# Two of three modulation rows summed on VectorE instead of TensorE, in a one-core DiT layer

## The reference, cut to what matters

```python
mod = (jax.nn.silu(c) @ w_mod[i] + b_mod[i])[:, None, :]     # 2048 x 12288
sh1, sc1, g1, sh2, sc2, g2 = jnp.split(mod, 6, axis=-1)
h = modulate(rms_norm(x, mix_norm_pre[i]), sh1, sc1)
p = h @ w_in[i]
...
x = x + g1 * rms_norm(mix @ w_out[i], mix_norm_post[i])
hf = modulate(rms_norm(x, ffn_norm_pre[i]), sh2, sc2)
x = x + g2 * rms_norm(swiglu(hf, w_gate[i], w_up[i], w_down[i]), ffn_norm_post[i])
```

## Time and profile before

| | us |
|---|---|
| median of 3 runs | 1610.84 (1610.16 to 1612.67) |
| profiled execution, its own time | 1613.92 |
| its span, first to last instruction | 1612.2 |
| TensorE matmul busy | 1538.3 (95%) |
| VectorE busy | 1033.4 (64%) |
| ScalarE busy | 739.2 (46%) |
| GpSimd busy | 222.2 (14%) |

### The profile page before, as it was taken

How to read it: one execution, slowest core, us unless ns; L and a number is a source line. 1 busy time by engine, 2 the same in 40 slices (tenths; PEclk the granted TensorE clock), 3 DMA queues, 4 the chain that set the end, 5 groups by cost and what they waited for, 6 DMA issues and landing times.

```text
span 1612.2 us, 25110 instructions
## 1 busy us (share of the span) xinstructions
PE 1538.3 (95%) x9297; PEld 1295.0 (80%) x9297; DVE 1033.4 (64%) x1435; ACT 739.2 (46%) x1042; POOL 222.2 (14%) x236
## 2 busy tenths in 40 slices
PE   3888999999999999999999999999999999999998
PEld 0557888898889888898877888888888888888786
DVE  1446899999997766665577544545454454777554
ACT  5535534443345745455357444444444443443332
POOL 2000223333242324244100000000000000000000
PEclk9998999999999999999999999999999999999999
DMA  9994566555655556564373766666666666998653
GB/s 351 382 397 116 167 199 196 190 190 183 208 179 176 171 171 209 170 196 132 118 261 117 212 194 186 192 185 192 184 193 192 187 190 191 339 321 319 222 187 136
DMA packets 190977, 334.58 MB, mean 208 GB/s; under 512 B 14706, under 2 KB 80354, under 8 KB 189985
## 3 DMA queue, kind: packets, MB, share of 16 engines
q1 hardware_dynamic: 190194, 330.89, 63.3%
q0 software_dynamic: 688, 2.39, 0.5%
HBM read 331.15 MB, written 2.10 MB: 207 GB/s over the span
## 4 chain that ended last, share of the span: by engine, by line
PE 82%; DVE 9%; DMA 2%; ACT 2%; SPq 2%; issue 2%; DVEq 0%; ACTq 0%
PE PS L1886 67%; DVE cacc L1752 3%; DMA first<-in_w_mod_dram 2%; DVE w_lo L1465 2%; PE PS L2107 2%; PE PS L2155 2%; PE PS L1892 2%; PE PS L2201 2%; SPq L756 2%; DVE sil L1586 1%; PE PS L2053 1%; PE PS L2097 1%; PE PS L1982 1%; DVE xyi L1645 1%; ACT L973 1%
## 5 line engine op out<-in xcount | busy, mean ns | idle before, releaser
L977 ACT ACTIVATE w_hi<-raw 128x1024 fp32r<-128x1024 f32 (+1 forms) x422 | 443.2, 1056 | 494.8 <-PE PS L1886 418.1
L1432 DVE TENSOR_TENSOR w_lo<-raw,w_hi 128x1024 fp32r<-128x1024 f32 x264 | 323.0, 1225 | 309.9 <-ACT w_hi L977 309.8
L1886 PE MATMUL PS<-w_hi,h_hi 128*128 128x512 f32 x704 | 275.2, 391 | 0.0
L1886 PE MATMUL PS<-w_hi,h_lo 128*128 128x512 f32 x704 | 274.3, 390 | 0.0
L1886 PE MATMUL PS<-w_lo,h_hi 128*128 128x512 f32 x704 | 274.1, 389 | 0.0
L1886 PE MATMUL PS<-h_hi,w_hi 128*128 128x256 f32 (+1 forms) x784 | 237.6, 303 | 0.0
L1465 DVE TENSOR_TENSOR w_lo<-raw,w_hi 128x1024 fp32r<-128x1024 f32 (+1 forms) x158 | 195.8, 1250 | 56.5 <-ACT w_hi L977 56.5
L1886 PE MATMUL PS<-h_hi,w_lo 128*128 128x256 f32 (+1 forms) x784 | 221.5, 283 | 0.0
L1886 PE MATMUL PS<-h_lo,w_hi 128*128 128x256 f32 (+1 forms) x784 | 221.4, 282 | 0.0
L1886 PEld LDWEIGHTS PS<-h_hi,w_hi 128*128 128x128 f32 (+1 forms) x784 | 148.3, 189 | 36.1 <-issue 32.0
L1886 PEld LDWEIGHTS PS<-w_hi,h_lo 128*128 128x128 f32 x704 | 132.3, 188 | 27.6
(11 more groups left out here) (323 smaller groups left out, 2338.4 us busy)
## 6 DMA issues: line engine op xcount, KB each, us to landing
raw<-in_w_in_dram SPq DMA_DIRECT2D x128, 512.0 KB, 3.8
raw<-in_w_mod_dram SPq DMA_DIRECT2D x96, 512.0 KB, 5.3
raw<-in_w_gate_dram SPq DMA_DIRECT2D x88, 512.0 KB, 3.6
raw<-in_w_up_dram SPq DMA_DIRECT2D x88, 512.0 KB, 3.6
raw<-in_w_down_dram SPq DMA_DIRECT2D x88, 512.0 KB, 4.6
first<-in_w_mod_dram SPq DMA_DIRECT2D x64, 512.0 KB, 9.3
raw<-in_w_out_dram SPq DMA_DIRECT2D x32, 512.0 KB, 4.3
gin<-in_w_mod_dram SPq DMA_DIRECT2D x32, 512.0 KB, 6.0
```

Of the source, the lines that this page charges most:

```text
L977: act.activation(out_ap, in_ap, ACT.Copy).then_inc(S[kind], 1)
L1432: dve.tensor_tensor(w_lo[:, slot, :], raw[:, (R0 + n) % RING, :], w_hi[:, slot, :].bitcast(F32), ALU.subtract).then_inc(S["lo"], 1)
L1886: ins = pe.matmul(out_ap, a[i], b[j], start=start and n == 0, stop=stop and n == 2, skip_group_check=grouped)
```

## The change

One row (`g1`) stays on TensorE, and its 16 steps `mrm` are spread at half the former pace, so that they end at two thirds of the main loop. The other two rows are cut into four quarters of 512 columns, each into 8 steps `md` on VectorE: one ring entry of 128 x (2 x 512), two dependent instructions that multiply by a column of `csil` and add to `mrw`. A quarter ends in `mcol`, four fp32 matmuls with `mrw` as weights and one column of ones, which also sum over the partitions, and in `mcc`. So there are 2 x 4 x 9 = 72 entries in the new list `rows`. They are placed by `beside()` one every 4 slots, once the convolution and row `g1` are done; what is left over is placed ahead of `WO_REST`, but for 9 entries, which go one ahead of each of its first units. The steps `md` wait for one another, and the first of a quarter waits for the `mcol` of the quarter before.

The two steps of each inverse root become one step with a counter of ScalarE's own, and the second load of `x` becomes a step `xin` of its own at the former place; `s2` moves behind the last entry of `rows`.

```diff
@@ make_plan
-    mr = [(grp, j) for grp in range(MR) for j in range(KT)]
+    mr = [(grp, j) for grp in range(MR - DR) for j in range(KT)]
+    rows = [x for grp in range(MR - DR, MR) for q in range(NQ) for x in [[("md", (grp, q, j))] for j in range(KT // 2)] + [
+        [("mcol", (grp, q)), ("mcc", (grp, q))]]]
@@ beside
+        if row_slot[0] is None and ("dw", (NP - 1, NDW - 1)) in placed and ("mcc", (MR - DR - 1,)) in plan:
+            row_slot[0] = slot[0] + AFTER["md0"]
+        if rows and row_slot[0] is not None and slot[0] >= row_slot[0]:
+            put(rows.pop(0))
+            row_slot[0] += AFTER["md"]
@@ gates and its call
+                if grp == MR - DR - 1:
+                    plan.extend([("mcol", (grp,)), ("mcc", (grp,))])
-            gates(MR * KT * done // total - (MR * KT - len(mr)))
+            gates((MR - DR) * KT * MR * done // (2 * total) - ((MR - DR) * KT - len(mr)))
@@ ahead of WO_REST
     until(("mix_lo", (NP - 1,)))
     assert not any(queue for _, queue in queues)
-    plan.append(("s2", ()))
+    while len(rows) > KT // 2 + 1:
+        put(rows.pop(0))
+    if not rows:
+        plan.append(("s2", ()))
+    plan.append(("xin", ()))
     for n, (c, kg) in enumerate(WO_REST):
         if n < 2:
             plan.extend([("gdiag", (0, 2 * n)), ("gdiag", (0, 2 * n + 1))])
         u = ("wo", c, kg)
+        if rows:
+            put(rows.pop(0))
+            if not rows:
+                plan.append(("s2", ()))
@@ SyncE: source of a ring entry
+            if u[0] == "md":
+                _, grp, q, j = u
+                col = (2 + grp) * D + 512 * q
+                return w_mod_v[:, 2 * j:2 * j + 2, col:col + 512]
@@ VectorE
+                elif kind == "md":
+                    grp, q, j = key
+                    n = at_ring[("md", *key)]
+                    dve.wait_ge(landed[n % RING], 16 * (n // RING + 1))
+                    if j == 0:
+                        need(dve, "mcol", *((grp, q - 1) if q else (grp - 1, NQ - 1) if grp > MR - DR else (grp - 1,)))
+                    for i in range(2):
+                        part, col = raw[:, n % RING, 512 * i:512 * (i + 1)], csil[:, LAT, 2 * j + i:2 * j + i + 1]
+                        if j or i:
+                            ins = dve.scalar_tensor_tensor(out=mrw[:, :], in0=part, scalar=col, in1=mrw[:, :],
+                                                           op0=ALU.mult, op1=ALU.add)
+                        else:
+                            ins = dve.tensor_scalar(mrw[:, :], part, col, None, ALU.mult)
+                        if i == 0:
+                            step(ins)
+                    ins.then_inc(done, 1)
+                    if j < KT // 2 - 1:
+                        need(dve, "md", *key)
@@ TensorE
+                elif kind == "mcol" and key[0] >= MR - DR:
+                    grp, q = key
+                    need(pe, "md", grp, q, KT // 2 - 1)
+                    b = aux(pe, kind, key)
+                    for n in range(4):
+                        ins = pe.matmul(PS[:, b, n:n + 1], mrw[:, P * n:P * (n + 1)], ones[:, 0:1], start=True, stop=True)
@@ ScalarE: inverse_root
+                n_chain[0] += 1
+                act.activation(log_ap, in_ap, ACT.Ln, bias=eps, scale=scale).then_inc(ch_act, 1)
+                act.wait_ge(ch_act, n_chain[0])
                 return act.activation(out_ap, log_ap, ACT.Exp, scale=-0.5)
```

More of the change, by code:

```diff
@@ L68 @@
 MR = 3
+DR = 2
 VC_MOD = 128
@@ L296, in make_plan @@
             for s in (CTX, LAT):
-                plan.extend([("xsq", (s, 0)), ("xsq", (s, 1)), ("xrt", (s,)), ("xrc", (s,)), ("xn", (s, 0)), ("xn", (s, 1))])
+                plan.extend([("xsq", (s, 0)), ("xsq", (s, 1)), ("xrc", (s,)), ("xn", (s, 0)), ("xn", (s, 1))])
         if n == 4:
@@ L320, in make_plan @@
             gates(len(mr))
-            plan.extend([("mcol", (MR - 1,)), ("mcc", (MR - 1,))])
         rest = [c[0] for c in STREAM[n:]]
@@ L350, in make_plan @@
         unit(("wo", c, kg), QS, beside)
-    assert not late and not soon
+    assert not late and not soon and not mr
     until(("mix_lo", (NP - 1,)))
     assert not any(queue for _, queue in queues)
-    plan.append(("s2", ()))
+    while len(rows) > KT // 2 + 1:
[3 more added lines that the diff above has]
+    plan.append(("xin", ()))
     for n, (c, kg) in enumerate(WO_REST):
@@ L370, in make_plan @@
     plan = splits_ahead(plan)
-    ring = [u for kind, key in plan if kind in ("hi", "mrm")
-            for u in ([key[0]] if kind == "hi" else [("mr", *key, 0), ("mr", *key, 1)])]
+    ring = [u for kind, key in plan if kind in ("hi", "mrm", "md")
+            for u in ([key[0]] if kind == "hi" else [("md", *key)] if kind == "md" else [("mr", *key, 0), ("mr", *key, 1)])]
     return plan, ring
 INTO_FFN = """
-    ysq 0 3, ysm 0, yg 0 3, yrt 0, yrc 0, mm 0 1, mm 0 3, mm 1 1, mm 1 3, mm 2 1, mm 2 3, mm 3 1, mm 3 3, xT 0 0,
+    ysq 0 3, ysm 0, yg 0 3, yrc 0, mm 0 1, mm 0 3, mm 1 1, mm 1 3, mm 2 1, mm 2 3, mm 3 1, mm 3 3, xT 0 0,
     xT 1 0, xT 2 0, mm 4 1, xT 3 0, xT 8 0, mm 4 3, mm 5 1, mm 5 3, mm 6 1, mm 6 3, mm 7 1, mm 7 3, xT 5 0, xT 3 1,
     ft 0 0, xT 5 1, xT 4 0, xT 6 0, xT 2 1, xT 0 1, xT 8 1, xT 1 1, xT 4 1, ft 1 0, ft 2 0, xT 7 1, xT 7 0, xT 6 1,
-    ft 3 0, ft 0 1, ft 1 1, ft 2 1, fh 0, psq 0 0, psq 0 1, xrt 0, xrc 0, fh 1, xTc 8 0, fm 2, fhi 0, fm 1, ysq 1 3, fhi 1,
-    yrt 1, yrc 1, fh 2, fhi 2, psq 1 0, psq 1 1, xrt 1, xrc 1, fh 3, xTc 8 1, fm 4, fhi 4, fhi 3, fm 5, fm 6, fhi 5, pn 0 1,
+    ft 3 0, ft 0 1, ft 1 1, ft 2 1, fh 0, psq 0 0, psq 0 1, xrc 0, fh 1, xTc 8 0, fm 2, fhi 0, fm 1, ysq 1 3, fhi 1,
+    yrc 1, fh 2, fhi 2, psq 1 0, psq 1 1, xrc 1, fh 3, xTc 8 1, fm 4, fhi 4, fhi 3, fm 5, fm 6, fhi 5, pn 0 1,
     pn 0 0, pn 0 3, pn 0 2, psm 0, xdg 0, fx 2, fx 1, fx 0, fv 0, flo 0, fl 0, ysm 1, yg 1 3, pn 1 1,
@@ L476, in layer @@
     SQUARED = {name: [step for step in PLAN if step[0] == name] for name in ("ysq", "psq")}
-    UNITS = [u for u in RINGED if u[0] != "mr"]
+    UNITS = [u for u in RINGED if u[0] not in ("mr", "md")]
     at_unit = {u: n for n, u in enumerate(UNITS)}
@@ L611, in sem @@
             return es.enter_context(nc.semaphore(name))
-        S = {kind: sem(f"s_{kind}") for kind in TOTALS if kind not in ("fh", "fl", "ft")}
+        S = {kind: sem(f"s_{kind}") for kind in TOTALS if kind not in ("xin", "fh", "fl", "ft")}
         S["fh"], S["fl"] = S["hi"], S["lo"]
@@ L762, in _ @@
                             small_in[f"x{i}"], 16)
-                elif kind in ("hi", "mrm"):
-                    for u in [key[0]] if kind == "hi" else [("mr", *key, 0), ("mr", *key, 1)]:
+                elif kind in ("hi", "mrm", "md"):
+                    for u in [key[0]] if kind == "hi" else [("md", *key)] if kind == "md" else [("mr", *key, 0), ("mr", *key, 1)]:
                         n = at_ring[u]
@@ L960, in _ @@
                     ins.then_inc(S[kind], 1)
-                elif kind == "s2":
+                elif kind == "xin":
                     need(pool, "mix_lo", NP - 1)
@@ L1514, in _ @@
                 elif kind == "s2":
-                    need(dve, "mcc", 2)
+                    need(dve, "mcc", MR - 1, NQ - 1)
                     dve.scalar_tensor_tensor(out=sc2[:, :], in0=modc[:, 2 * KT:3 * KT], scalar=1.0,
@@ L1773, in _ @@
                     dve.tensor_tensor(cacc[:, :, :], cacc[:, :, :], bc(cx[:, 0, :], 1, 8), ALU.mult).then_inc(done, 1)
+                elif kind == "md":
[16 more added lines that the diff above has]
+                        need(dve, "md", *key)
+                elif kind == "mcc" and key[0] >= MR - DR:
+                    grp, q = key
+                    need(dve, "mcol", *key)
+                    at = KT * grp + 4 * q
+                    dve.tensor_tensor(modc[:, at:at + 4], PS[:, BANK["mcol", key], 0:4],
+                                      vcol[:, VC_MR + at:VC_MR + at + 4], ALU.add).then_inc(done, 1)
                 elif kind == "mcc":
```

89 lines of the change are left out of this document (31 added, 58 removed).

## The result

The changed kernel takes **1664.51 us** (median of 4 runs, 1661.95 to 1665.25) against 1611.76 (4 runs, 1610.16 to 1612.85): ratio 1.0326, 95% interval 1.0313 to 1.0339. The forecast was 1618.8 with a range of 1605 to 1629. The direction was right; the loss is 53 us, not 8. The time is outside the range. The profiled execution took 1665.25 us, its span is 1663.5.

The account below looks back on a forecast made before the run. Up to 486 us TensorE and VectorE were both taken as full, from 530 to 746 TensorE alone. The terms -5 - 2 - 8 + 1.5 + 17 + 4.5 gave +8.0 us on the median 1610.8: 1618.8, range 1605 to 1629.

Parts of the forecast that it names:

- (a): Up to 486 us, end of the convolution: fewer TensorE steps, but VectorE nearly full; 5 us gained, between 1 and 9.
- (b): From 486 to 530 us, before the new list may start: 5 TensorE steps become 2 or 3; 2 us gained.
- (c): From 530 to 746 us, to the input projection's end: 16 TensorE steps go, 39 entries come; 8 us gained, 3 to 14.
- (d): `WO_FIRST`, 66 us: 12 `md` on VectorE and one `mcol` on TensorE; 1.5 us lost, 0 to 4.
- The relief behind 486 us: TensorE time saved behind the convolution, taken at full price: 2 us in (b), 15.5 us of steps in (c).
- rival 3: VectorE becomes the bound from 530 to 812 us, `md` blocks delaying the solve; +20 us, 1631; chance 0.18.
- (e): Ahead of `WO_REST`: 10 entries at once, TensorE stalls between two `mcol` with nothing to cover it; 17 us lost, 13 to 20.
- (f): `WO_REST`: eight units each get an `md` and a second ring entry, reloading slows them; 4.5 us lost, 1 to 9.
- At nothing: Merged inverse roots, `xin`, later `s2` and ring length put at zero; turned side-bank order given no sign, up to 2 us.
- The signs named ahead: Trace features said to confirm or refute terms, such as a TensorE gap of 14 us or more ahead of `WO_REST`.

Follow-up runs that it names:

- e5: The changed kernel with the 32 steps taken from TensorE put back as idle ones without loads; 1667.8 us, ratio 1.0341 to the kernel before.
- the two sets of kernels: Five kernels with a relieved TensorE up to the convolution's end and eleven with full load; they end it at 482.8 and 482.7 us in the mean.
- e13: e1 plus 32 extra VectorE steps of two dependent instructions each, without loads or `mcol`; 1630.4 us, ratio 1.0124 to the kernel before.
- e12: e1 plus 32 extra VectorE steps of one instruction each, without loads or `mcol`; 1615.7 us, ratio 1.0031 to the kernel before.
- e2: The changed kernel without the 72 entries, so two rows are not computed and TensorE's relief stays; 1599.0 us, ratio 0.9925 to the kernel before.
- e4: The changed kernel with each `md` working on 8 of its 512 columns, loads and waits kept; 1637.5 us, ratio 1.0175 to the kernel before.
- e14: The changed kernel with only one row on VectorE, plus 16 idle steps on TensorE; 1629.1 us, ratio 1.0112 to the kernel before.
- e1: The changed kernel with all rows back on TensorE at the old pace, merged roots and `xin` kept; 1611.4 us, ratio 1.0001 to the kernel before.

## Why the forecast was wrong

**(a) to 486 us, -5: wrong, nothing (+1.1, within the scatter).** That VectorE bounds the stretch was seen, yet half the chain's share was credited (the trace has 28 steps there, not 27). e5 and the means of the two sets of kernels show 0. The 9.25 us of idle time that VectorE has there were not to be had.

**(b), (c), (d), -8.5: this failed; +18.7.** The step is "There VectorE fills 96.7% and TensorE 96.0%; 202 / 0.967 = 209 ... I take 208". The prices were nearly right: a pair is 1.53 us quiet (831.66), and 2 x 0.943 = 1.89 in this stretch (1.76 forecast), which is some 4 us of VectorE over 35 `md`; an `mcol` is 0.95 (0.8 forecast). The capacity was wrong. With 85% of VectorE busy and TensorE not relieved the way to the junction is already 16 us longer (e13), and TensorE waits for steps of the chains, not for the rows. The first 29 us on VectorE cost 3 to 5 us, the next 30 cost 13 to 15 (e12, e13); whether the load or the length of a block does it stays open. The 53 entries cost 33 us against e2, some 20 of them VectorE's own time (e4), where the sum held about 10. The 97% was carried over from a stretch in which convolution steps fill VectorE. Why they fit there is my reading and no run shows it: they have slack, while the steps behind 530 us depend on each other across engines at set slots, and VectorE works in order.

**The relief behind 486 us, some 18 in the sum: 13.6 where nothing else is added and the loads are gone too** (e2), and 0.4 to 0.55 of TensorE's time beside the `md` (e5, e14). Gains and losses don't add up one by one: rival 3 reckoned with this in kind ((c) gains 3, (d) loses 4) but priced it at +20 in all. It comes nearest to what the runs show, at a price far too small.

**(e), +17: the mechanism exactly as read, +19.9 on the path, 22.1 of TensorE idle.** Eight pairs with one wait for a load take 14.25 us (835.17 to 849.42), against 12.3 and some 3 for loads; that the load of `x` shares the DMA then was in the forecast, and e4 bears it out. Missed were 4.1 us: entry 53 waits for the late `md` of slot 565, which stands behind `hc_lo` and `w_lo` on VectorE. And an `mcol` takes 1.8 us at half the clock, twice. After TensorE has idled from 829.1 the clock is 0.50 to about 856 us; the sum had no term for it.

**(f), +4.5 (1 to 9): +11.7**, from the start of `WO_REST` to ffn 63.5 us instead of 51.8. Of it 2.5 are the first unit at half clock (5.26 in place of 2.72), 5.5 the last `mcol` with its wait (3.67 and 1.86); a second spell at half clock follows at 887 to 891 us, worth 2. The slow reloading of the ring was not the main part.

**At nothing: right** for the roots and `xin` (e1); the turned order of the side banks wasn't tested by itself. **The signs named ahead:** the gap of 14 us or more with 16 instructions in it is there; the pair at 1.53 is there; "if VectorE is under 90% busy from 530 to 746 us, (c) is wrong" came true, in the other sense than meant: it is at 87%, and slower.

The range ended at 1629, short even of rival 3's 1631. Rival 3 had the stretch from the convolution to the junction at -1 ((b) -2, (c) -3, (d) +4); it is +18.7. At the junction and behind it rival 3 had 26, the runs 31.6; the late `md` (4.1) and the clock (some 6: 2 for two `mcol`, 2.5 for the first unit, 2 for the spell at 887) are more than the missing 5.6, so its other terms were 4 or 5 too high.

## What to carry to other kernels

An engine that takes part in a chain of short dependent steps can have far less room than its idle time says: here the first 29 us of added work, to 75% busy, cost 0.1 to 0.2 us per us, and the next 30 cost 0.44 to 0.5. To price work that is moved onto such an engine, put idle steps of that length there (e12, e13) before the work itself is moved. Time taken off the other engine was worth only 0.4 to 0.55 of its size once the chain was late. And a burst with a wait at its end, at a place where TensorE has nothing else, is paid in full and once more in the clock; look there at what the DMA carries at the same moment.
